# Three more gate projections as seven half-size products, and three small moves after them

## The chip, the cores and the metric

One core of one Trainium2 chip runs one program. The time is device microseconds of that program, the median over several executions. The engines are TensorE (PE in the profile; its weight loads are PEld), VectorE (DVE), ScalarE (ACT), GpSimd (POOL) and SyncE (SP), which here only issues the large weight transfers. Everything is float32.

## What is computed

Two transformer-like blocks run one after the other on a sequence of 256 tokens with 1024 channels. The first block is the one that the change touches:

```python
z = (x @ w_in).astype(F32)
zA, zB, zC, zD, zG = _split(z[..., :N_COLS_BASE], (RWKV_COLS, HGRN_COLS, MLSTM_COLS, LRU_COLS, GATE_COLS))
yA, v_cur = rwkv7_mix(zA, ...)        # four token mixers A, B, C, D
yB, yC, yD = hgrn2_mix(zB, ...), mlstm_mix(zC, ...), rglru_mix(zD, ...)
gates = jax.nn.sigmoid(zG).reshape(bsz, seq, N_BRANCH, D_MODEL)
merged = jnp.zeros((bsz, seq, D_MODEL), F32)
for n, yb in enumerate((yA, yB, yC, yD)):
    merged = merged + gates[:, :, n] * (yb @ w_branch[layer, n])
x = _layernorm(DEEPNORM_ALPHA * x + merged @ w_out[layer], ...)
# then a mixture of 32 experts and a second block with windowed attention
```

## The kernel before

**Units.** The input projection is cut into units of 512 output columns ("B g", "G D 0", "G D 1" and so on; `UNITS`, line 147). A unit's weights are 128 x 8 x 512 floats, 2 MB. They lie in a ring of three places: SP starts the transfer of unit n once unit n-3 has been multiplied (lines 680 to 690, `unit_used`). PE works through the units in the order of the list, and the small matmuls of the four mixers stand between them.

**A unit in the plain form** is `ones_channels` (line 944): two banks of 16 matmuls, each 128 x 128 weights against 256 tokens, 32 in all. ACT copies each bank out (`out`, line 2083).

**A unit in seven products** is Strassen's scheme on 2 x 2 quarters. `early_product` (line 1151) is eight matmuls, 128 x 128 weights against 128 tokens; `early_1` to `early_7` are the seven products P1 to P7 with their waits, 56 matmuls in all. POOL makes the four sums of weight quarters T1 to T4 (`first_sums`, `last_sum`, `in_pieces`, lines 849 to 873), DVE makes the sums of token quarters once for all units (`token_sums`, line 2478). One PSUM bank, U, collects P1, P6, P5 and P3 in turn; ACT copies it out after each (`split_copy`, line 2225: C11 after P1, C21 after P6, C22 after P5, C12 after P3), and DVE adds P2 to C11, P7 to C22 and P7 with P4 to C21 (`c11`, `c22`, `c21`). Four units are done so before: "G B 0", "G B 1", "G A 0", "G A 1" (`EARLY`, line 151). The order in which products, copies and additions are counted is written out in `split_run`, `copy_run` and `add_run` (lines 513 to 523), and must be the order on PE, ACT and DVE.

**The stretch around the three units.** PE runs B i, the small matmul `ada(3)`, B g, the four "C num" banks, G D 0, G D 1, the transposes "C yT", the four banks of `merge("D")` ("Wb D"), "B diag", and then a loop of eight levels with a unit of A between them. ACT and DVE run B's logarithm, its running sum (`tensor_tensor_scan`), and C's normalization at the same time.

**The stretch around the small moves.** A loop `for l in range(1, 5)` builds A's inverse: PE does X{l}, D{l} and DT{l} in 64 x 64 matmuls (lines 1276 to 1311 stand for the small ones of this loop and the merges), with products of G B 0 and G B 1 between them, and DVE copies each result back (lines 2780, 2793, 2803). A table of attention biases for the second block is made on the way, and ACT stores it, 128 times repeated (4.6 MB), to DRAM: `act.dma_start(scratch...)`, line 2223, after the copies of "A Kt". `y_gated` on DVE waits for that store, since its output lies over the table, and SP waits for it before the second block. The bonus term of A is scaled on DVE after X5 (lines 2813 to 2815). At the end of A come G A 0 and G A 1, with the two turns `y_turned(0)` and `y_turned(1)` near the last products, and then `merge("A")`, which needs both halves of A's output ("A_done", from `y_gated`).

Of the kernel before, what the change touches and what calls it, by code (L numbers as in the profile page):

```python
# [7 lines left out]
ALU = mybir.AluOpType  # L8
# [4 lines left out]
P = 128  # L13
# [137 lines left out]
EARLY = ["G B 0", "G B 1", "G A 0", "G A 1"]  # L151
START = len(EARLY)
QKV = [f"{c}{g}" for g in range(GROUPS) for c in "QKV"]
# [66 lines left out]
def build(nc, ins, consts, outs):  # L220
    stack = ExitStack()
    with stack:
# [249 lines left out]
        def split_weights(u):  # L472
# [3 lines left out]
            if u < START:  # L476
                t1, t2, t4 = (room(FREE + 1024 * n, 4, T) for n in range(3))
            elif u > ENDS:
                at_ = RING + SUMS_SLOT * UNIT + u % 2 * 1024
                t1, t2, t4 = room(at_, 4, T), room(at_ + 2048, 4, T), room(FREE + 2048, 4, T)  # L480
            else:
                t1, t2, t4 = spare_w[u % 2]
# [9 lines left out]
        def split_bank(u, which):  # L492
# [6 lines left out]
            else:  # L499
                name = {"U": f"{odd if u % 2 else even} 0", "P2": f"{even} 1", "P7": f"{odd} 1"}[which]  # L500
# [12 lines left out]
        split_run = [(x, u) for u in range(START) for x in ("P1", "P2", "P6", "P7", "P5", "P3", "P4")]  # L513
        split_run += [("P1", START), ("P2", START)] + [x for u in range(START, ENDS + 1) for x in split_turn(u)]
        split_run += [(x, u) for u in LATER for x in ("P1", "P2", "P6", "P7", "P5", "P3", "P4")]
        copy_run = [(x, u) for u in range(START) for x in ("C11", "C21", "C22", "C12")]
# [17 lines left out]
        def split_out(u, i, j):  # L534

            name = SPLIT[u]
            if u < START:
# [282 lines left out]
        def _(pool):  # L820
# [19 lines left out]
            pool.wait_ge(sig("proj_full"), proj_no("A g 1") + 1)  # L840
            for dst, src in ((RELB, ins["rel_bias_2"]), (HOT, consts["hot"]), (TAB, consts["mask"])):
                pool.dma_start(dst, src).then_inc(sig("table_loaded"), 16)
            def mask(l):

                pool.wait_ge(sig("NTm_early"), 4)
                pool.wait_ge(sig("small_full"), small_no(f"A X{l - 1} 1") + 1)
                pool.tensor_tensor(NTm, NT, along(c("level64", l * CH, l * CH + CH), 16), ALU.mult).then_inc(sig("NTm_ready"), 1)

# [25 lines left out]

            mask(2)
            first_sums(0)
            mask(3)
            last_sum(0)
            mask(4)
            first_sums(1)  # L880
            mask(5)
            last_sum(1)
# [4 lines left out]
            for u in range(2, START):  # L887
# [36 lines left out]
        def _(pe):  # L924
# [121 lines left out]
            ones_channels("B g")  # L1046
# [16 lines left out]
            ones_channels("G D 0")  # L1063
            ones_channels("G D 1")
# [10 lines left out]
            turned("C yT", hC.rearrange("p (j h) e -> p j (h e)", j=TT), "C_normed")  # L1075
            merge("D")
# [15 lines left out]
            for l in range(8):  # L1092
# [10 lines left out]
                else:  # L1103
# [3 lines left out]
                    mm.then_inc(sig("small_full"), 1)  # L1107
                if l < 7:
# [41 lines left out]

            def early_product(u, bank, a_name, b_name, first):

                a, b = split_tokens(a_name, SUMS1), split_weights(u)[b_name]
                for m in range(2):
                    for k in range(4):
                        cols = slice(m * P, m * P + P)
                        mm = pe.matmul(split_bank(u, bank)[:, cols], b[:, k, cols], a[:, k, :], start=first and m == 0 and k == 0, stop=k == 3,  # L1157
                                       skip_group_check=True)
                mm.then_inc(sig("split_full"), 1)

            def early_1(u):

                unit(SPLIT[u])
                if u == 0:
                    pe.wait_ge(sig("proj_out"), proj_no("A Kt 1") + 1)
                if u > 1:
                    pe.wait_ge(sig("split_copied"), copied_out("C12", u - 2))
                early_product(u, "U", "A11", "B11", True)

            def early_2(u):  # L1170

                if u:
                    pe.wait_ge(sig("split_added"), added_up("C11", u - 1))
# [2157 lines left out]
```

## Time and profile before

| | |
|---|---|
| median of 3 runs | 1722.17 us (1720.59 to 1722.74) |
| the profiled execution, its own time | 1723.5 us |
| its span in the trace | 1721.7 us |
| PE busy | 1692.8 us, 98% of the span |
| DVE, ACT, POOL busy | 605.9, 271.5, 130.6 us |
| mean granted TensorE clock | 0.998 of full speed |

1.8 us of the profiled time lie outside the span. The timeline lists groups of instructions: start, length, engine, line, operation, sizes, count, and in brackets the idle time before the group and what ended it. A float32 matmul is two records, so 32 matmuls are "x64". Ends of matmuls are modelled and overlap the next start; from start to start is what a group costs.

### The profile page before, as it was taken

The page shows a single profiled execution, that of the slowest core. Times are in us where ns is not written, and L with a number is a line of the kernel's source. Part 1 is how long each engine was busy: PE and PEld are TensorE (multiplying, and loading weights), DVE is VectorE, ACT ScalarE, POOL GpSimd, SP SyncE. Part 2 cuts the span into 40 slices and gives each one's busy share as a digit, 9 for nine tenths or more (in the row PEclk, how much of TensorE's full clock was granted, in tenths as well). Part 3 has the DMA queues.
Part 4 walks back from the last instruction along what each step waited for, and adds up shares of the span by engine and source line. Part 5 has one row for each costly group of instructions (what it writes and reads, how often), then busy time and mean ns, then how long its engine had stood idle before and what let it go on. Part 6 is the DMA issues. An engine that isn't in the chain of part 4 may idle for free.

```text
span 1721.7 us, 25566 instructions
## 1 busy us (share of the span) xinstructions
PE 1692.8 (98%) x10669; PEld 1009.5 (59%) x10669; DVE 605.9 (35%) x1116; ACT 271.5 (16%) x477; POOL 130.6 (8%) x181
## 2 busy tenths in 40 slices
PE   9999999999999999999999999999999999999998
PEld 8787888889553333333434333333333337999995
DVE  4684467456341211111111111112111126454773
ACT  1323115001011111110101010101001112111231
POOL 1000000552000000000000000000000000005600
PEclk9999999999999999999999999999999999999999
DMA  8564332554979999999999999999999997443251
GB/s 320 190 258 166 147 123 100 166 167 185 378 319 423 406 428 428 427 429 428 428 429 428 426 429 427 427 430 427 426 430 427 427 416 297 161 178 117 99 191 48
DMA packets 61975, 540.60 MB, mean 314 GB/s; under 512 B 5192, under 2 KB 12136, under 8 KB 32452
## 3 DMA queue, kind: packets, MB, share of 16 engines
q1 hardware_dynamic: 56160, 528.42, 74.7%
q10 hardware_dynamic: 3956, 5.86, 1.2%
q0 software_dynamic: 1776, 5.10, 0.9%
q8 instruction: 67, 1.10, 0.3%
q14 instruction: 16, 0.13, 0.0%
HBM read 533.57 MB, written 5.78 MB: 313 GB/s over the span
## 4 chain that ended last, share of the span: by engine, by line
PE 92%; DMA 3%; DVE 2%; ACT 1%; issue 1%; SPq 0%; DVEq 0%; ACTq 0%
PE small L1654 24%; PE small L1693 13%; PE proj L1865 11%; PE proj L956 11%; PE proj L1630 3%; PE small L1596 3%; PE proj L1157 3%; PE small L1642 2%; PE small L1661 2%; PE small L976 2%; PE proj L965 2%; PE proj L1140 2%; PE small L1793 2%; PE small L2062 2%; PE small L1519 2%; DMA arena<-in_expert_w_down 1%
## 5 line engine op out<-in xcount | busy, mean ns | idle before, releaser
L1654 PE MATMUL small<-arena 128*64 128x512 f32 x2048 | 446.2, 593 | 2.3 <-DMA arena<-in_expert_w_gu 1.0
L1654 PEld LDWEIGHTS small<-arena 128*64 128x64 f32 x2048 | 151.5, 137 | 281.3 <-issue 276.0
L1693 PE MATMUL small<-arena 128*64 128x512 f32 x1024 | 227.0, 595 | 8.3 <-ACT arena L2288 7.4
L3024 DVE TENSOR_SCALAR arena<-small 128x512 f32<-128x512 f32 x32 | 22.1, 691 | 533.8 <-PE small L1661 533.8
L1865 PE MATMUL proj<-arena 128*128 128x128 f32 x1680 | 192.7, 276 | 0.0
L1865 PEld LDWEIGHTS proj<-arena 128*128 128x128 f32 x1680 | 189.4, 192 | 3.3 <-issue 2.5
L956 PE MATMUL proj<-arena 128*128 128x256 f32 x832 | 183.0, 380 | 0.0
L956 PEld LDWEIGHTS proj<-arena 128*128 128x128 f32 x832 | 157.1, 190 | 22.0 <-issue 0.5
L1693 PEld LDWEIGHTS small<-arena 128*64 128x64 f32 x1024 | 74.3, 137 | 139.5 <-issue 138.4
L852 POOL TENSOR_TENSOR arena<-arena 128x256 f32<-128x256 f32 x144 | 104.5, 759 | 159.3 <-PE proj L1865 98.8
L2283 ACT ACTIVATE arena<-arena 128x512 f32<-128x512 f32 x32 | 20.2, 630 | 490.3 <-DVE arena L3024 490.3
L899 POOL DMA_DIRECT2D arena<-shape_poolcnt x1 | 0.5, 538 | 962.1 <-PE proj L1630 962.1
L2229 ACT ACTIVATE arena<-proj 128x256 f32<-128x256 f32 x76 | 29.1, 383 | 267.6 <-PE proj L1865 161.7
L1630 PE MATMUL proj<-arena 64*128 64x512 f32 x256 | 63.6, 615 | 0.8 <-ACT arena L2323 0.8
L3037 DVE TENSOR_TENSOR arena<-arena 128x128 f32 x16 | 4.7, 292 | 168.1 <-ACT arena L2307 168.1
L1596 PE MATMUL small<-arena 128*64 128x512 f32 x256 | 62.0, 605 | 0.0
L2083 ACT ACTIVATE arena<-proj 128x512 f32<-128x512 f32 (+2 forms) x54 | 30.8, 592 | 186.3 <-PE proj L956 130.8
L2467 DVE TENSOR_TENSOR arena<-proj,arena 128x256 f32<-128x256 f32 x57 | 24.2, 424 | 98.6 <-PE proj L1865 58.5
L1157 PE MATMUL proj<-arena 128*128 128x128 f32 x448 | 55.4, 282 | 0.1
L1157 PEld LDWEIGHTS proj<-arena 128*128 128x128 f32 x448 | 52.6, 196 | 1.2 <-ACT arena L2229 0.3
L2293 ACT ACTIVATE arena<-small 128x512 f32<-128x512 f32 x31 | 18.5, 597 | 208.9 <-PE small L1693 208.9
L3123 DVE TENSOR_TENSOR arena<-arena 128x1024 f32<-128x1024 f32 x40 | 49.0, 1225 | 4.2 <-DVE arena L2467 3.1
(461 smaller groups left out, 1618.3 us busy)
## 6 DMA issues: line engine op xcount, KB each, us to landing
arena<-in_expert_w_gu SPq DMA_DIRECT2D x128, 2048.0 KB, 19.3
arena<-in_expert_w_down SPq DMA_DIRECT2D x47, 2048.0 KB, 27.0
arena<-in_w_in_first SPq DMA_DIRECT2D x20, 2048.0 KB, 8.6
arena<-in_w_in SPq DMA_DIRECT2D x15, 2048.0 KB, 8.1
arena<-in_expert_w_down SPq DMA_DIRECT2D x17, 1536.0 KB, 29.1
arena<-in_w_ada SPq DMA_DIRECT2D x6, 2048.0 KB, 12.7
arena<-in_expert_w_down SPq DMA_DIRECT2D x17, 512.0 KB, 30.7
arena<-in_w_branch SPq DMA_DIRECT2D x4, 2048.0 KB, 8.6
```

The costliest lines, as they stand in the source:

```text
L852: op = pool.tensor_tensor(dst[:, k, :], a[:, k, :], b[:, k, :], ALU.subtract)
L956: mm = pe.matmul(ps[:, m * T:m * T + T], lhs, XT[:, k, :], start=k == 0, stop=k == KD - 1)
L965: mm = pe.matmul(ps[:, :], XT[:, k, j * P:j * P + P], w[:, k, :], start=k == 0, stop=k == KD - 1)
L976: mm = pe.matmul(ps[:, m * T:m * T + T], w[:, k, (2 * i + m) * P:(2 * i + m + 1) * P], YT[b][:, k, :], start=k == 0, stop=k == KW - 1)
L1140: mm = pe.matmul(ps[:, m * T:m * T + T], w[:, k, quarter * P:quarter * P + P], XT[:, k, :], start=k == 0, stop=k == KD - 1)
L1157: mm = pe.matmul(split_bank(u, bank)[:, cols], b[:, k, cols], a[:, k, :], start=first and m == 0 and k == 0, stop=k == 3, skip_group_check ...
L1596: mm = pe.matmul(bank[CAP * half:CAP * half + CAP, :], PICK[:, j, :], x1[:, j, half * W:half * W + W], start=j == 0, stop=j == 1, skip_gro ...
L1630: mm = pe.matmul(acc_bank[2 * j + half][:, :], PTW[lo:lo + CAP, j * P:j * P + P], YSB[lo:lo + CAP, :], start=first, stop=False, skip_group ...
L1654: mm = pe.matmul(bank[CAP * half:CAP * half + CAP, :], XG[:, k % 4, k // 4, :], w[:, k % 4, n * D + half * W:n * D + half * W + W], start= ...
L1693: mm = pe.matmul(bank[CAP * half:CAP * half + CAP, :], h[:, m, u, :], w[:, half * W:half * W + W], start=u == 0 and m == 0, stop=u == 1 an ...
L1865: mm = pe.matmul(split_bank(u, bank)[:, cols], lhs, rhs, start=first and m == 0 and k == 0, stop=k == 3, skip_group_check=True)
L3123: do(TTn(w[dst], w[a], w[b], op), "split_weights")
```

## The change

1. "B g", "G D 0" and "G D 1" go from the plain form to seven products each, with POOL making their weight sums at the point of its queue ahead of the table loads. `token_sums` on DVE moves ahead of B's logarithm. The products of D's two units are staggered: GD1's P1 stands before GD0's P3, and P3 and P4 of the last unit stand behind the turn of C. B g's P3 and P4 stand behind "C num".
2. ACT's store of the bias table moves from behind "A Kt" to behind the gates of G B 1.
3. DVE's scaling of the bonus moves from behind X5 into turn l = 4 of the loop, between the copies of X4 and the addition of D4.
4. The last product P4 of G A 1 moves behind `y_turned(1)` on PE, and on DVE `y_normed(1)` goes ahead of `y_gated(0)` and `c21` of G A 1 behind `y_gated(1)`.

```diff
-EARLY = ["G B 0", "G B 1", "G A 0", "G A 1"]
+EARLY = ["B g", "G D 0", "G D 1", "G B 0", "G B 1", "G A 0", "G A 1"]
...
+            for u in (BG, GD0, GD1):
+                first_sums(u)
+                last_sum(u)
             pool.wait_ge(sig("proj_full"), proj_no("A g 1") + 1)
...
             ones_tokens("B i")
             ada(3)
-            ones_channels("B g")
...
+            early_1(BG)
+            early_2(BG)
+            early_6(BG)
+            early_7(BG)
+            early_5(BG)
             pe.wait_ge(sig("C_weights"), 1)
...
-            ones_channels("G D 0")
-            ones_channels("G D 1")
+            early_3(BG)
+            early_4(BG)
+            early_1(GD0)
+            early_2(GD0)
+            early_6(GD0)
+            early_7(GD0)
+            early_5(GD0)
+            early_1(GD1)
+            early_3(GD0)
+            early_4(GD0)
+            early_2(GD1)
+            early_6(GD1)
+            early_7(GD1)
+            early_5(GD1)
...
             turned("C yT", hC.rearrange("p (j h) e -> p j (h e)", j=TT), "C_normed")
+            early_3(GD1)
+            early_4(GD1)
             merge("D")
...
-            early_3(3)
-            early_4(3)
+            early_3(GA1)
             y_turned(1)
+            early_4(GA1)
             merge("A")
...
             channels("B q", qB)
+            for j in range(TT):
+                out(f"B i {j}", vB[:, j, :])
+            split_copy(BG, "P1", 0, 0)
             act.wait_ge(sig("B_absf"), 1)
             do(act.activation(cB, cB, ACT.Exp, scale=-1.0))
             do(act.activation(cB, cB, ACT.Ln, bias=1.0), "B_ln")
-            for j in range(TT):
-                out(f"B i {j}", vB[:, j, :])
-            channels("B g", gB)
-            act.wait_ge(sig("proj_out"), proj_no("B g 1") + 1)
+            split_copy(BG, "P6", 1, 0)
             do(act.activation(tB, qB, ACT.Sigmoid))
+            split_copy(BG, "P5", 1, 1)
             do(act.activation(kB, fB0, ACT.Sigmoid, scale=-1.0))
+            split_copy(BG, "P3", 0, 1)
+            act.wait_ge(sig("split_copied"), copied_out("C12", BG))
+            act.wait_ge(sig("split_added"), added_up("C21", BG))
             do(act.activation(eB, gB, ACT.Sigmoid), "B_sig")
+            act.nop().then_inc(sig("proj_out"), 2)
+            split_copy(GD0, "P1", 0, 0)
             log_and_exp()
...
+            early_gate(GB1)
             act.wait_ge(sig("table_done"), 1)
             act.dma_start(scratch.rearrange("p h c -> h p c"), along(TAB, P)).then_inc(sig("table_stored"), 16)
...
             dve.nop().then_inc(sig("C_weights"), 1)
+            token_sums(SUMS1)
...
+            c11(BG)
             differences(0)
+            c22(BG)
...
             do(TTn(hC, hC, over(stC[:, 0, :], P), ALU.mult))
+            c21(BG)
...
+                else:
+                    for ct in range(4):
+                        do(STT(bonusA[:, ct, :], bonusA[:, ct, :], pv("rwkv_lnx_b", ct, ct + 1), gA[:, ct, :], ALU.add, ALU.mult))
+                    do(TTn(gA, gA, over(pv("rwkv_lnx_g"), T), ALU.mult))
                 for i in range(TT):
                     do(TTn(Dv[:, i], tiles(full(f"A D{l} {i}"), CH), Dv[:, i], ALU.add), "small_out")
...
-            y_gated(0)
             y_normed(1)
-            c21(3)
+            y_gated(0)
             y_gated(1)
+            c21(GA1)
             merge("A", False)
```

## Rows read from the trace of the kernel before

**Rows 1.** The page: the busy time of the engines.

```profile
PE 1692.8 (98%) x10669; PEld 1009.5 (59%) x10669; DVE 605.9 (35%) x1116; ACT 271.5 (16%) x477; POOL 130.6 (8%) x181
```

**Rows 2.** Waits of PE up to 480 us: waiter, releaser, us, times, longest.

```profile
PE small L1300 <- issue: 3.2, 1, 3.2
PE small L976 <- DVE arena L2886: 1.6, 1, 1.6
PE small L1300 <- DVE arena L2749: 0.8, 1, 0.8
```

**Rows 3.** Timeline of PE: B g, and what follows it.

```profile
141.75 14.06 PE L956 MATMUL proj<-arena 128*128 128x256 f32 x64
155.65 1.06 PE L1057 MATMUL small<-arena 128*128 128x129 f32 x8
```

**Rows 4.** Timeline of PE: two of the seven products, and what follows them.

```profile
328.00 3.84 PE L1157 MATMUL proj<-arena 128*128 128x128 f32 x32
331.67 1.04 PE L1311 MATMUL small<-arena 128*128 128x128 f32 x8
```

**Rows 5.** Timelines of DVE, ACT and POOL: what the three units' chain is made of.

```profile
147.08 2.87 DVE L2619 TENSOR_TENSOR_SCAN arena<-arena 128x256 f32<-128x256 f32 x4
...
159.89 1.22 DVE L2645 TENSOR_TENSOR arena<-arena 128x1024 f32<-128x1024 f32 x1
...
143.57 1.06 ACT L2152 ACTIVATE arena<-arena 128x1024 f32<-128x1024 f32 x1 [18.19 <-DVE arena L2615]
...
330.15 0.38 ACT L2229 ACTIVATE arena<-proj 128x256 f32<-128x256 f32 x1 [23.52 <-PE proj L1157]
...
408.27 12.20 POOL L852 TENSOR_TENSOR arena<-arena 128x256 f32<-128x256 f32 x16 [33.56 <-PE proj L1157]
```

**Rows 6.** Timeline of PE around the longest gap, in turn l = 4.

```profile
353.45 1.04 PE L1300 MATMUL small<-arena 64*64 64x64 f32 x54
...
358.34 3.37 PE L1157 MATMUL proj<-arena 128*128 128x128 f32 x16
361.55 1.04 PE L1311 MATMUL small<-arena 128*128 128x128 f32 x8
```

**Rows 7.** Windows: each engine's busy us (instructions), PEclk, DMA share, GB/s.

```profile
330.00:340.00 10.00, 10.00 (x185) 9.69 (x186) 3.33 (x7) 1.15 (x3) 2.42 (x2) 1.00 0.86 284
...
380.00:390.00 10.00, 10.00 (x251) 8.75 (x251) 6.54 (x12) 0.00 (x0) 0.00 (x0) 1.00 0.01 3
...
358.00:359.00 1.00, 1.00 (x13) 0.88 (x10) 0.64 (x1) 0.00 (x0) 0.00 (x0) 0.50 1.09 354
```

**Rows 8.** Timeline of ACT: the issue of the bias table's store.

```profile
323.66 0.35 ACTq L2223 DMA_DIRECT2D bias_rows<-arena  x1
```

**Rows 9.** DMA, 344 to 345 and 366 to 367: weight loads, KB each, us to landing.

```profile
arena<-in_w_in_first SPq DMA_DIRECT2D x1, 2048.0 KB, 15.9
...
arena<-in_w_in_first SPq DMA_DIRECT2D x1, 2048.0 KB, 8.5
```

**Rows 10.** DMA queues, 354 to 358 and 358 to 362: packets, MB, share.

```profile
q8 instruction: 1, 0.02, 1.4%
...
q10 hardware_dynamic: 211, 0.31, 20.5%
```

**Rows 11.** Timeline of DVE: the bonus, the same operation elsewhere, the copies of X4.

```profile
216.32 1.01 DVE L2687 SCALAR_TENSOR_TENSOR arena<-arena 128x256 f32<-128x256 f32 x2
...
349.88 1.42 DVE L2780 COPY arena<-small 128x512 f32<-128x512 f32 x2 [0.69 <-PE small L1289]
...
368.82 3.63 DVE L2814 SCALAR_TENSOR_TENSOR arena<-arena 128x256 f32<-128x256 f32 x4
372.49 1.63 DVE L2815 TENSOR_TENSOR arena<-arena 128x1024 f32<-128x1024 f32 x1
```

**Rows 12.** Timeline of DVE ahead of `merge("A")`.

```profile
427.89 0.69 DVE L2879 TENSOR_TENSOR arena<-arena 128x512 f32<-128x512 f32 x1
...
429.79 0.42 DVE L2467 TENSOR_TENSOR arena<-proj,arena 128x256 f32<-128x256 f32 x1 [1.21 <-PE proj L1157]
```

More of the change, by code:

```diff
@@ L499, in split_bank @@
             else:
-                name = {"U": f"{odd if u % 2 else even} 0", "P2": f"{even} 1", "P7": f"{odd} 1"}[which]
+                name = {"U": f"{odd if (u - START) % 2 else even} 0", "P2": f"{even} 1", "P7": f"{odd} 1"}[which]
             return proj_bank[proj_no(name) % 4]
@@ L885, in _ @@
             pool.dma_start(bcb, ins["ln1_b"][0].partition_broadcast(P)).then_inc(sig("ln1_loaded"), 16)
-            for u in range(2, START):
+            for u in (GA0, GA1):
                 first_sums(u)
@@ L1045, in _, with early_product @@
             ada(3)
-            ones_channels("B g")
+            def early_product(u, bank, a_name, b_name, first):
+                a, b = split_tokens(a_name, SUMS1), split_weights(u)[b_name]
+                for m in range(2):
+                    for k in range(4):
+                        cols = slice(m * P, m * P + P)
+                        mm = pe.matmul(split_bank(u, bank)[:, cols], b[:, k, cols], a[:, k, :], start=first and m == 0 and k == 0, stop=k == 3,
+                                       skip_group_check=True)
+                mm.then_inc(sig("split_full"), 1)
@@ new lines, in early_5, with early_3, early_4 @@
+            def early_5(u):
+                pe.wait_ge(sig("split_copied"), copied_out("C21", u))
+                early_product(u, "U", "S1", "T1", False)
+            def early_3(u):
+                pe.wait_ge(sig("split_copied"), copied_out("C22", u))
+                early_product(u, "U", "S4", "B22", False)
+            def early_4(u):
+                pe.wait_ge(sig("split_weights"), 4 * u + 4)
+                pe.wait_ge(sig("split_added"), added_up("C22", u))
+                early_product(u, "P7", "A22", "T4", False)
+                for _ in range(2):
+                    pe.nop().then_inc(sig("proj_full"), 1)
@@ L2809, in _ @@
                     dve.nop().then_inc(sig("table_done"), 1)
[L2810 removed]
+            c21(GB1)
             for i in range(TT):
                 do(TTn(X[:, 8 * i:8 * i + 8, :], tiles(full(f"A X5 {i}"), CH), along(c("eye64"), 8), ALU.add), "small_out")
[L2813 to L2815 removed]
             merge("B", False, (0,))
```

261 lines of the change are left out of this document (132 added, 129 removed).

## The prediction

> **What bounds the kernel now.** First the page: PE is busy for 1692.8 us of a span of 1721.7, and the next engine for 605.9 [rows 1]. So the time is PE's work plus its gaps, 28.9 us in all. An edit pays if it shortens PE's work or closes a gap of PE; work on any other engine costs nothing until PE waits for it. Second, the waits of PE in the first 480 us, where the whole change lies: 3.2 us on "issue" (nothing that the trace shows), 1.6 us for the last half of A's output, and 0.8 us for a copy behind the bonus [rows 2]. Third, the timeline of PE around B g: the groups follow one another with no idle time [rows 3], so there only PE's own work can be saved, and every new wait is paid in full.
>
> **Seven products for three units.** A plain unit of 64 records runs from 141.75 to 155.65, that is 13.90 us [rows 3]. Two products of eight matmuls, 32 records, run from 328.00 to 331.67, that is 3.67 us or 1.835 each [rows 4]; seven are 12.85. The saving is 1.05 us a unit, 3.15 for three. It is small because half the tokens per matmul don't give half the time (0.229 us against 0.434): seven eighths of the arithmetic would be 12.16, and 0.69 us of each unit is lost to the shorter matmul.
>
> What the products wait for, by hand from 141.75. POOL needs 12.2 us for the four sums of a unit [rows 5]. Those of B g start when its weights land, about 136, and are done before the products that read them. Those of G D 0 start with the end of B g's P5 (141.75 + 5 x 1.835 = 150.9) and T2 is there after half of them, at 157.0, while PE comes to P6 of G D 0 only at 141.75 + 9 x 1.835 + 2.7 for "C num" = 160.9. So POOL hides, with 4 us to spare. For G D 1 the spare is 7.3 - 6.1 = 1.2 us: four products lie between P5 of G D 0 and P6 of G D 1.
>
> DVE and ACT are the tighter chain. ACT can copy P1 of G D 0 out only after B's last sigmoid, which now needs the whole of B g, its last addition C21 among it, and DVE does that addition only after B's logarithm and C's division. From 142.2 on DVE: token sums 2.8 (four of 512 elements, at 1.22 for 1024 [rows 5]), absolute value 1.2, then ACT 2 x 1.1 [rows 5], then DVE 1.2, scans 2.9 [rows 5], C11 0.4, differences 1.4, C22 0.4, eight copies of "C num" 2.4, small ones 0.8, the division 1.2, C21 0.5: 159.8 to 160.3. ACT's sigmoid 1.1 and the copy 0.4 [rows 5] give 161.8 to 162.1. PE wants it at 160.9, so P6 of G D 0 waits about 1.1 us. Behind it on PE stands everything else, so it is paid. The lower bound is 0.9. The upper one takes each of some six two-operand operations of that chain longer by 0.4, as the bonus is at 368.82 while POOL works (0.908 each against 0.505) [rows 11]: 3.5. I take 1.2, since POOL is idle in most of that chain (B g's sums end near 148). Later copies, C's turn and the gates of D have several us of room, and D's merge follows as before. Sum of part 1: -3.15 + 1.2 = **-1.9** (-2.3 to +0.4).
>
> The page "SBUF — State Buffer" of the Trainium skill, section "SBUF: two separate sides", says that a DVE operation with two SBUF inputs and a GpSimd one lock each other out for a whole instruction. Rows 11 agree with it (0.4 us more each). By it every unit's 16 POOL operations could hold DVE up; the sum above is bounded by the rows and doesn't need it.
>
> **The store of the bias table.** ACT issues it at 323.66 [rows 8]; 211 of its packets still move between 358 and 362 [rows 10]. While it runs, a weight load takes 15.9 us to land, and one issued at 366 takes 8.5 [rows 9]. In the midst of one group of D4, after 54 of 64 records, PE stands still for 3.24 us on "issue" [rows 2, 6]. No semaphore stands inside that group, and the next packet of the instruction queue is the one that moves between 354 and 358 [rows 10]: I read it as PE out of instructions, whose fetch is behind the store and the stretched weight load. The clock then goes from 1.00 to 0.50 (2.4 to 1.2 GHz) [rows 7], and a product takes 3.21 us instead of 1.835 [rows 6], 1.4 more. The gap and its clock are **4.6 us**. With the store issued some 44 us later (about 367, behind G B 1's gates), that place has a load of 8.5 us only. I take all 4.6 as gained there; the other end is 0, if the weight load alone is enough.
>
> The store is moved, not removed. It then runs from about 368 to 395, at first beside the load of G A 1, which is needed at 414 and has room, and PE's instructions go faster there: 251 records in 380 to 390 against 185 in 330 to 340 [rows 7]. Something of the same kind may come back. Bounds are 0 (with the store and a load together at 330 to 340, DMA share 0.86, PE had no gap [rows 7]) and 4.6 once more; I take **+0.7**. The wait of DVE for the store in `y_gated`, at about 427, has 30 us of room, and `merge("B")` and the loads behind are not queued on ACT. ACT's queue gains nothing else.
>
> The page "Runtime: NRT & Kernel Launch", section "Instruction fetch mechanics", of the Trainium skill says that instructions come in blocks of 16 KiB by a queue of the engine's own, and that a crossing is mostly hidden. By that rule the gap of 3.24 us would have another cause and part 2 would be worth 0. Rows 6 and 10 speak against "hidden": one packet of the instruction queue falls into the gap.
>
> **The bonus sooner.** The four operations and the multiplication take 3.63 + 1.63 = 5.3 us with POOL busy, 4 x 0.505 + 1.2 = 3.2 without [rows 11]. At their new place DVE is free from 351.3 (end of the copies of X4, 349.88 + 1.42 [rows 11]) until PE ends D4. POOL is busy there too. So DVE ends at 354.5 to 356.6, and the two additions of D4 (1.4) at 356.1 to 358.1. PE runs D4 from 353.45 for 1.1 and one product of 1.8 behind it, and wants the result at 356.4: a new wait of 0 to 1.8, and behind it on PE stand DT4 and all the rest. I take **+1.2**. At the old place the wait of 0.8 goes [rows 2]: **-0.8**. Next late there is PE itself, with no gap before 431.
>
> **The last product behind the second turn.** PE waits 1.6 us for A_done before `merge("A")` [rows 2]. On DVE, C21 of G A 1 at 429.79 waited 1.21 us for P4 with the last `y_gated` behind it, and `y_normed(1)` at 427.89 stood behind `y_gated(0)` [rows 12]. Now DVE does the norm at about 426.5, PE turns it after P3, near 427.8, and P4 fills the next 1.8 us while DVE does four operations of 0.7, done near 430.0, just as P4 ends. **-1.5** (-1.6 to -0.8). The addition C21 and its sigmoid are late by 2 us, but the merge needs that half of the gate only 7 us later.
>
> **Sum**: -1.9 - 4.6 + 0.7 + 1.2 - 0.8 - 1.5 = -6.9 us. The profiled execution of 1723.5 becomes 1716.6, and the median of 1722.2 becomes 1715.3 us. The profiled execution is 1.3 above the median; I keep the difference and not its time.
>
> **Rivals.**
> (a) The fetch gap comes back once under the moved store, or stays at 354 because the load alone makes it. For it: PE's instructions are denser there [rows 7], and I can't see from outside where a block ends. Against it: the store ran beside a load at 330 to 340 with no gap. -6.9 - 0.7 + 4.6 = -3.0: 1719.2. The rule of the Runtime page leads to the same time by another way.
> (b) The three units cost more than they save: the chain over B g's C21 is longer, because POOL's sums stretch DVE's operations, or G D 1's sums come late (1.2 us of room). The wait is then 3.5 for the first and about 2 for the second, part 1 is +2.4 instead of -1.9, and the time 1719.6.
> (c) Slower: the gap comes back several times. The place is 372 to 395, where PE uses its instructions 251/185 = 1.36 times as fast with the store in every DMA engine's queue. At 4.6 us each, three of them give -7.6 + 13.8 = +6.2: 1728.4. It decides from 11.0 us of new gaps on (7.6 to make good, 3.4 for the bound). Against it: even in the old place there was one gap in 38 us of store.
> (d) The moves don't do what they say: the clock and the gap are a matter of one execution and not of the median. The three runs spread over 2.2 us, less than the 4.6, so the gap is in all or in none; if it is in none, -2.3: 1719.9.
>
> **Chances.** Forecast 0.58; (a) 0.18; (b) 0.08; (c) 0.06; (d) 0.10. What this kernel's measurement can tell from no change is about 0.2%, 3.4 us: faster is below 1718.7. The forecast's own range, 1712.0 (no wait anywhere: -3.15 + 0.9 - 4.6 - 0.8 - 1.6, less 1 for what I can't see) to 1718.7, is faster; of (a), (b) and (d), whose centres lie 1 us on the other side, about one in six is. Faster 0.63, same 0.30, slower 0.07. The range that should hold it 8 times in 10 takes in those three centres with 2 us above them: 1712.0 to 1721.7.
>
> **What would show each step.** Seven products of about 1.83 us for each of the three units, with one gap of about 1 us before P6 of G D 0, released by ACT's copy; "C yT" and "Wb D" start 2 us sooner. No "issue" gap near 350, PEclk 1.00 from 350 to 362, and the load of G A 0 landing in 8.5 us. A gap of about 1 us before DT4, released by DVE. No wait before DT5, and at most 0.3 before `merge("A")`. It is wrong if an "issue" gap of over 2 us stands between 365 and 400, if DVE's operations near 150 to 160 are much above their lengths of rows 5, or if a weight load after 366 makes PE wait.

## The result: slower by 0.6%, and the profile after

The changed kernel takes 1732.43 us (median of 4 runs, 1729.07 to 1734.59) against 1721.38 for the kernel before (4 runs, 1719.80 to 1722.74): a ratio of 1.0064, 95% interval 1.0052 to 1.0076, that is 9.0 to 13.1 us. The forecast was 1715.3 with a range of 1712.0 to 1721.7. The profiled execution is the shortest of the four, 1729.07 us with a span of 1727.3.

First the waits of PE up to 480 us, which answer to [rows 2] (waiter, releaser, us, times, longest):

```profile
PE small L1454 <- issue: 2.9, 1, 2.9
PE proj L1062 <- ACT arena L2190: 2.6, 1, 2.6
PE small L1347 <- DVE arena L2856: 1.8, 1, 1.8
PE proj L1062 <- issue: 1.6, 1, 1.6
PE proj L1062 <- POOL arena L850: 1.6, 1, 1.6
PE proj L1062 <- DVE arena L2517: 1.5, 1, 1.5
...
PE small L1508 <- issue: 0.9, 1, 0.9
PE proj L1062 <- DVE arena L2531: 0.3, 1, 0.3
```

The three waits of [rows 2] were 5.6 us together. They are gone from their places, and eight others of 13.2 us stand there. Five of them are L1062, the seven products of the three units. The timeline of PE behind B g's first five products, which answers to [rows 3]:

```profile
154.73 1.95 PE L1062 MATMUL proj<-arena 128*128 128x128 f32 x16
158.19 5.60 PE L1062 MATMUL proj<-arena 128*128 128x128 f32 x48 [1.52 <-DVE arena L2517]
166.42 14.37 PE L1062 MATMUL proj<-arena 128*128 128x128 f32 x112 [2.63 <-ACT arena L2190]
182.40 2.02 PE L1062 MATMUL proj<-arena 128*128 128x128 f32 x16 [1.61 <-issue]
185.98 3.84 PE L1062 MATMUL proj<-arena 128*128 128x128 f32 x32 [1.56 <-POOL arena L850]
189.66 1.04 PE L1161 MATMUL small<-arena 128*128 128x128 f32 x8
190.53 3.74 PE L1062 MATMUL proj<-arena 128*128 128x128 f32 x32
194.10 6.21 PE L986 MATMUL small<-arena 128*128 128x256 f32 x28
```

Read the gaps by what stands behind them: 158.19 is P4 of B g, waiting for the addition C22; 166.42 is P6 of G D 0, waiting for ACT's copy of its P1; 182.40 is P6 of G D 1 (the wait has no releaser in the records; in the experiment without sums below it is gone) and 185.98 its P7, waiting for POOL's T2 and T3. The merge of D begins at 194.10, 51.9 us behind B g's start (142.19), where it was 45.1. And the later part, with a window of 395 to 398 (busy us of PE, PEld, DVE, ACT, POOL with instructions, PEclk, DMA share, GB/s):

```profile
365.66 1.09 PE L1347 MATMUL small<-arena 128*128 128x128 f32 x8 [1.78 <-DVE arena L2856]
...
398.08 1.27 PE L1454 MATMUL small<-arena 64*64 64x64 f32 x34 [2.86 <-issue]
...
437.66 2.64 PE L986 MATMUL small<-arena 128*128 128x256 f32 x11
...
395.00:398.00 3.00, 0.21 (x7) 0.08 (x3) 0.67 (x1) 0.00 (x0) 0.00 (x0) 1.00 0.94 238
```

The gap near 355 [rows 6] is gone, and one of the same kind, in the midst of a group of 64 records and with the DMA queues full, stands at 398. The merge of A at 437.66 has no wait any more.

### The profile page after: what moved, and what is told of

It is laid out like the page before. It is cut to its first block, busy times and chain, and to the rows that moved or that the text cites. A ratio compares the mean times of both kernels' runs of the same rounds, so it can differ in the third digit from the quotient of the medians.

```text
span 1727.3 us, 25957 instructions
## 1 busy us (share of the span) xinstructions
PE 1691.2 (98%) x10813; PEld 1011.5 (59%) x10813; DVE 615.4 (36%) x1125; ACT 274.4 (16%) x485; POOL 169.7 (10%) x229
## 4 chain that ended last, share of the span: by engine, by line
PE 91%; DVE 4%; DMA 1%; ACT 1%; issue 1%; POOL 1%; DVEq 0%; ACTq 0%; POOLq 0%
PE small L1690 25%; PE small L1729 13%; PE proj L1901 11%; PE proj L966 8%; PE proj L1666 3%; PE small L1632 3%; PE proj L1062 3%; PE small L1678 2%; PE small L1697 2%; PE small L1312 2%; PE small L986 2%; PE proj L975 2%; PE proj L1233 2%; PE small L1829 2%; PE small L2098 2%; PE small L1555 2%
## 5 line engine op out<-in xcount | busy, mean ns | idle before, releaser
L1901 PE MATMUL proj<-arena 128*128 128x128 f32 x1680 | 192.7, 276 | 0.0
L850 POOL TENSOR_TENSOR arena<-arena 128x256 f32<-128x256 f32 x192 | 143.6, 781 | 203.3 <-PE proj L1901 101.0
L966 PE MATMUL proj<-arena 128*128 128x256 f32 x640 | 141.0, 380 | 0.0
L1062 PE MATMUL proj<-arena 128*128 128x128 f32 x784 | 95.3, 280 | 7.7 <-ACT arena L2190 2.6
L1062 PEld LDWEIGHTS proj<-arena 128*128 128x128 f32 x784 | 91.1, 195 | 9.8 <-issue 6.2
L2190 ACT ACTIVATE arena<-proj 128x256 f32<-128x256 f32 x88 | 33.7, 383 | 293.4 <-PE proj L1901 161.7
L2517 DVE TENSOR_TENSOR arena<-proj,arena 128x256 f32<-128x256 f32 x66 | 28.0, 425 | 106.6 <-PE proj L1901 58.9
L2119 ACT ACTIVATE arena<-proj 128x512 f32<-128x512 f32 (+2 forms) x48 | 27.3, 591 | 174.3 <-PE proj L966 103.7
## 6 DMA issues: line engine op xcount, KB each, us to landing
arena<-in_w_ada SPq DMA_DIRECT2D x6, 2048.0 KB, 12.2
```

The costliest lines, as they stand in the source:

```text
L850: op = pool.tensor_tensor(dst[:, k, :], a[:, k, :], b[:, k, :], ALU.subtract)
L966: mm = pe.matmul(ps[:, m * T:m * T + T], lhs, XT[:, k, :], start=k == 0, stop=k == KD - 1)
L1901: mm = pe.matmul(split_bank(u, bank)[:, cols], lhs, rhs, start=first and m == 0 and k == 0, stop=k == 3, skip_group_check=True)
```

## The experiments

Two theories at first. **P**: the three units lose by POOL's sums, which are late themselves and stretch DVE's operations. **F**: the moved store starves PE of instructions at its new place. The texts written ahead of the runs also name rivals: **W**, the whole loss is PE's new waits between 142 and 190 us; **Q**, the order of ACT's and DVE's queues makes them; **M**, the moved bonus makes the loss of the three moves. The kernels ran in three groups of four, in the order of the table, each group on one chip (three chips in all) beside the kernel before; it took 1721.11 (26 runs), 1721.17 (31) and 1720.85 us (26).

| kernel | median us (lowest to highest, runs) | ratio, 95% interval |
|---|---|---|
| the three moves alone | 1727.58 (1721.01 to 1731.06, 10) | 1.0036, 1.0021 to 1.0051 |
| the products alone | 1727.14 (1725.31 to 1729.05, 5) | 1.0038, 1.0024 to 1.0053 |
| products, no sums on POOL | 1718.54 (1716.24 to 1719.56, 10) | 0.9987, 0.9978 to 0.9997 |
| products, queues reordered | 1721.62 (1719.17 to 1725.68, 10) | 1.0006, 0.9996 to 1.0015 |
| store alone | 1725.79 (1719.12 to 1729.86, 10) | 1.0027, 1.0009 to 1.0045 |
| bonus alone | 1720.44 (1719.25 to 1723.36, 10) | 0.9994, 0.9980 to 1.0007 |
| last product alone | 1718.13 (1716.99 to 1722.87, 10) | 0.9988, 0.9977 to 0.9999 |
| three moves, store of 32 rows | 1720.95 (1720.05 to 1722.26, 10) | 1.0002, 0.9992 to 1.0012 |
| before, store of 32 rows | 1718.87 (1718.16 to 1720.07, 10) | 0.9992, 0.9983 to 1.0002 |
| two units | 1716.99 (1714.58 to 1720.10, 10) | 0.9978, 0.9966 to 0.9991 |
| two units, store of 32 rows | 1714.66 (1714.33 to 1715.32, 7) | 0.9966, 0.9954 to 0.9977 |
| the change, store of 32 rows | 1723.67 (1722.75 to 1726.17, 8) | 1.0020, 1.0009 to 1.0031 |

### The two halves of the change

The three moves (store, bonus, last product) on the kernel before; and the changed kernel with the three moves undone. Both are cut from the diff of the change as it stands; of the first, the store:

```diff
                 out(f"A Kt {i}", Kt[:, i, :])
-            act.wait_ge(sig("table_done"), 1)
-            act.dma_start(scratch.rearrange("p h c -> h p c"), along(TAB, P)).then_inc(sig("table_stored"), 16)
...
             early_gate(1)
+            act.wait_ge(sig("table_done"), 1)
+            act.dma_start(scratch.rearrange("p h c -> h p c"), along(TAB, P)).then_inc(sig("table_stored"), 16)
             act.wait_ge(sig("merged"), 3)
```

> The kernel before with the three later moves alone (store later, bonus sooner, last product behind the second turn); no unit is changed. Theory W (the loss comes from PE's new waits between 142 and 190 us, and the moves gain a little): the profiled span falls by about 1.3 us against 1721.7, since from 328 to 431 the changed kernel ran 1.34 us shorter than the one before (lead of 7.28 us at the first product of G B 0, 5.94 at the merge of A), and the median lies 0.5 to 2.5 us below before's. Theory F (the moved store leaves PE without instructions in another place in each execution, and this makes the median of the changed kernel worse by 11 us where its profiled execution is worse by 5.6): the median is 3 to 6 us above before's, and the trace has an 'issue' gap of 2 to 6 us between 365 and 400.

> The three units as seven products, and none of the three later moves. Theory W: the merge of D starts 7.3 us later than in the kernel before (194.1 against 186.8), as in the changed kernel, with the waits 0.3, 1.5, 2.6, 1.6 and 1.6 us on PE before it; the span and the median are 6 to 8 us above before's, and the 3.2 us gap on issue stands in the loop as it did or at another place nearby. Theory F: the median is only 5 to 7 us above, and the rest of the 11 us is missing because the store is back at its old place.

Measured: +6.5 and +6.0 us. Each half loses by itself, and together they are near the change's +11. In the profile of the moves alone the gap on "issue" is 3.30 us, at another place (381.73), and the executions lie 10 us apart. In that of the products alone the merge of D comes 50.3 us behind B g's start.

### The products without POOL's sums

```diff
-                in_pieces(w["T1"], w["B12"], w["B11"])
+                in_pieces(w["T1"], w["B12"], w["B11"], u < GB0)
```

> The three units as seven products without the later moves, and POOL's sums of weights for these three units left out (each sum is one memset of one column instead of four subtractions; the products read rooms that are not sums). Theory P (POOL is the cause: its sums come late for G D 1, and its work stretches DVE's operations): the waits of PE on POOL (1.6 us twice) go, DVE's operations between 150 and 185 have their old lengths (differences 0.69, the division 1.22), the chain of B g's C21 is about 3 us shorter, and of the 7.3 us lead at the merge of D 5 to 7 go. Theory Q (the order of the queues is the cause: ACT's copy of G D 0 stands behind a sigmoid that wants the whole of B g, and DVE's addition C22 stands behind the scans and the differences): the waits of 1.5 and 2.6 us stay at over half their size, and only the two on POOL go: the lead falls by about 3.5 us.

`u < GB0` sets the argument `light` of `in_pieces` for the three units: one small memset then stands in place of the four operations of each sum. The products read rooms that hold no sums, so this kernel doesn't compute the block; it is built for its times alone.

The timeline of PE, and two rows of DVE (the differences of B):

```profile
162.01 18.10 PE L1067 MATMUL proj<-arena 128*128 128x128 f32 x160 [1.22 <-ACT arena L2195]
...
184.40 1.89 PE L991 MATMUL small<-arena 128*128 128x256 f32 x8
...
153.17 0.69 DVE L2688 TENSOR_TENSOR arena<-arena 128x512 f32<-128x512 f32 x1
153.90 0.69 DVE L2689 TENSOR_TENSOR arena<-arena 128x512 f32<-128x512 f32 x1
```

With POOL idle one gap is left, 1.22 us ahead of P6 of G D 0, and the stretch takes 184.40 - 141.58 = 42.8 us, 2.3 less than before. The gaps ahead of P6 and P7 of G D 1 are gone with the sums. POOL's sums, and what they stretch on DVE, are all that was taken out, so the wait of P6 is put down to T2, though the records name no releaser. Theory P holds for the products: the same instructions on PE gain 2.3 us without POOL's work and lose 5.2 with it. What POOL does to DVE stands in the trace of the changed kernel:

```profile
151.06 3.64 DVE L2670 TENSOR_TENSOR_SCAN arena<-arena 128x256 f32<-128x256 f32 x4
...
155.19 1.27 DVE L2683 TENSOR_TENSOR arena<-arena 128x512 f32<-128x512 f32 x1
156.49 1.10 DVE L2684 TENSOR_TENSOR arena<-arena 128x512 f32<-128x512 f32 x1
...
158.28 0.42 DVE L2692 COPY arena<-small 128x256 f32<-128x256 f32 x1
...
160.90 0.72 DVE L2695 SCALAR_TENSOR_TENSOR arena<-arena 128x8 f32<-128x8 f32 x1
...
162.57 1.59 DVE L2698 TENSOR_TENSOR arena<-arena 128x1024 f32<-128x1024 f32 x1
...
164.72 1.06 ACT L2213 ACTIVATE arena<-arena 128x1024 f32<-128x1024 f32 x1 [7.56 <-DVE arena L2517]
165.89 0.38 ACT L2190 ACTIVATE arena<-proj 128x256 f32<-128x256 f32 x1
...
152.36 13.76 POOL L850 TENSOR_TENSOR arena<-arena 128x256 f32<-128x256 f32 x16 [8.11 <-PE proj L1062]
173.79 14.99 POOL L850 TENSOR_TENSOR arena<-arena 128x256 f32<-128x256 f32 x16 [7.68 <-PE proj L1062]
```

The differences take 1.27 and 1.10 us instead of 0.69, the scans 3.64 instead of 2.87 [rows 5], an operation of eight elements 0.72 instead of 0.17 (another, at 158.08, keeps its 0.17), and POOL's 16 operations 13.8 and 15.0 instead of 12.2 [rows 5]. The copies out of PSUM at 158.28 keep their 0.42. The page "SBUF — State Buffer" of the Trainium skill, section "SBUF: two separate sides", says that a DVE operation with two SBUF inputs and a GpSimd one that reads SBUF keep each other out for a whole instruction. The trace agrees: the operations above that grew have both inputs in SBUF, and the copies have none there.

### Queues reordered

ACT copies P1 of G D 0 ahead of B's last sigmoid; DVE does B g's additions C11 and C22 ahead of B's logarithm and differences, and C21 ahead of C's division. Nothing is added or removed.

```diff
+            split_copy(GD0, "P1", 0, 0)
             act.wait_ge(sig("split_copied"), copied_out("C12", BG))
             act.wait_ge(sig("split_added"), added_up("C21", BG))
             do(act.activation(eB, gB, ACT.Sigmoid), "B_sig")
             act.nop().then_inc(sig("proj_out"), 2)
-            split_copy(GD0, "P1", 0, 0)
```

> The three units as seven products without the later moves, POOL's sums as they are, and the queues put in another order: ACT copies P1 of G D 0 ahead of B's last sigmoid, DVE does C11 of B g in its idle time before B's logarithm, C22 ahead of the differences, and C21 ahead of C's division. Theory Q: the waits of 1.5 and 2.6 us go, with the half clock behind the second one (about 1.4 us), and the merge of D starts about 5 us earlier than in the run with the products alone; the waits on POOL stay or grow, since the sums of G D 1 still start with the end of P5 of G D 0. Theory P: other waits of the same size take their place, and the merge of D starts less than 2 us earlier.

```profile
170.91 5.62 PE L1062 MATMUL proj<-arena 128*128 128x128 f32 x48 [2.42 <-ACT arena L2190]
177.03 2.02 PE L1062 MATMUL proj<-arena 128*128 128x128 f32 x16 [0.49 <-issue]
181.07 3.84 PE L1062 MATMUL proj<-arena 128*128 128x128 f32 x32 [2.01 <-POOL arena L850]
...
189.19 3.19 PE L986 MATMUL small<-arena 128*128 128x256 f32 x14
```

The gaps of 1.52 and 2.63 us are gone, and one of 2.42 is there in their place: ACT's copy of P5 stands behind its wait for C's variance, as it did before the reordering, and PE now comes to it first. From B g's start (141.70) to the merge of D it is 47.5 us, 2.8 less than with the products alone, still 2.4 more than before. G D 1 still waits for its sums; an order of queues doesn't help that.

### The moves one by one

On the kernel before, the store as in the diff above; the bonus:

```diff
-                if l == 3:
+                elif l == 3:
                     c22(0)
+                else:
+                    for ct in range(4):
+                        do(STT(bonusA[:, ct, :], bonusA[:, ct, :], pv("rwkv_lnx_b", ct, ct + 1), gA[:, ct, :], ALU.add, ALU.mult))
+                    do(TTn(gA, gA, over(pv("rwkv_lnx_g"), T), ALU.mult))
...
-            for ct in range(4):
-                do(STT(bonusA[:, ct, :], bonusA[:, ct, :], pv("rwkv_lnx_b", ct, ct + 1), gA[:, ct, :], ALU.add, ALU.mult))
-            do(TTn(gA, gA, over(pv("rwkv_lnx_g"), T), ALU.mult))
             merge("B", False, (0,))
```

and the last product, on PE and then on DVE:

```diff
             early_3(3)
-            early_4(3)
             y_turned(1)
+            early_4(3)
...
-            y_gated(0)
             y_normed(1)
-            c21(3)
+            y_gated(0)
             y_gated(1)
+            c21(3)
```

> The kernel before with one move alone: the store of the bias table is issued behind G B 1's sigmoid (about 364 instead of 324 us). Nothing else is changed. Theory F (PE runs out of instructions behind the store, once or more, wherever the store runs): a gap of PE on "issue" of 2 to 4 us at a new place between 370 and 395, none near 354; a median some 4 to 7 us above before, about 1726 (1723 to 1730), and executions that lie several us apart, as with the three moves together (1721.0 to 1731.1). Rival M (the loss of the three moves is that of the bonus and of what waits behind it): 1721 or, with the old gap of 4.6 us closed, down to 1716.5, and executions within 3 us.

> The kernel before with the scaling of the bonus alone moved to the fourth turn of the loop. It takes PE's wait of 0.8 us at DT5 away and makes one of about 1.8 us before DT4 (measured with the three moves together). Theory F: +1.0, so 1722.1 (1721 to 1723.5), executions within 3 us of each other. Rival M: 1725 or more, with another wait of PE behind it.

> The kernel before with the product P4 of G A 1 alone moved behind the second turn of y. The wait of 1.6 us before the merge of A goes, and nothing takes its place: -1.5 us, 1719.6 (1719 to 1720.5). Rival: the merge waits for the gate's half that now comes 2 us later, or nothing is gained because the merge's weights or DVE are as late: 1721.1.

The store alone is the loss of the three moves: +4.6 us in the median, with executions from 1719.1 to 1729.9. The profiled execution (1723.15) shows one large gap (a second is 0.17) and, in the window behind it, the granted clock near half (1.2 of 2.4 GHz):

```profile
377.04 0.41 PE L1398 MATMUL small<-arena 64*64 64x64 f32 x8
380.60 3.14 PE L1398 MATMUL small<-arena 64*64 64x64 f32 x53 [3.14 <-issue]
...
382.00:384.00 2.00, 2.00 (x47) 2.00 (x45) 0.73 (x2) 0.00 (x0) 0.00 (x0) 0.53 0.75 169
```

The bonus alone (-0.7) can't be told from no change. In its trace neither wait of DVE stands: a gap on "issue" of 1.86 in D4 lies over the bonus. The last product alone gives -3.0 in the median with an interval from -4.0 to -0.2; its wait of 1.6 us is gone, and -1.6 lies within the interval.

### A smaller store

The table's 128 rows in memory are all the same row; the load reads each one column further back. Four loads of 32 partitions, each with its own start, need 32 rows: 1.2 MB to store and not 4.7 (128 rows of 24 x 384 floats; the 4.6 MB given at the start is a little low).

```diff
-            act.dma_start(scratch.rearrange("p h c -> h p c"), along(TAB, P)).then_inc(sig("table_stored"), 16)
+            act.dma_start(scratch.rearrange("p h c -> h p c"), along(TAB, 32)).then_inc(sig("table_stored"), 16)
...
-                    tab = bass.AP(tensor=scratch.tensor, offset=P - 1, ap=[[24 * BKT - 1, P], [BKT, 24], [1, T]])
-                    sp.dma_start(HK, tab).then_inc(sig("hankel_loaded"), 16)
+                    for a in range(4):
+                        tab = bass.AP(tensor=scratch.tensor, offset=P - 1 - 32 * a, ap=[[24 * BKT - 1, 32], [BKT, 24], [1, T]])
+                        sp.dma_start(HK[32 * a:32 * a + 32], tab).then_inc(sig("hankel_loaded"), 16)
```

> The three moves as in the run with all of them, but the moved store writes 32 rows of the bias table instead of 128 (1.2 MB instead of 4.7), and four loads of 32 partitions read them later; the result is the same table. Theory F: with a store of some 7 to 10 us in place of 27 PE's instructions come in time: no gap on "issue" over 1 us between 350 and 400, so -4.6 (the old gap) +1.0 (bonus) -1.5 (last product) = -5.1, about 1716 (1715 to 1719), and executions within 3 us of each other. Rival: the gaps aren't the store's but those of the place (64x64 matmuls use up instructions too fast) or of the bonus's wait: about 1727 as with the full store, or at least a gap of 2 us or more in the profile.

The waits of PE, up to 480 us and behind:

```profile
PE small L1312 <- DVE arena L2798: 1.8, 1, 1.8
...
PE proj L1866 <- DMA arena<-in_w_in: 1.7, 1, 1.7
```

No gap on "issue" between 350 and 400, and the executions lie 2.2 us apart and not 10: as theory F has it. The median, 1720.95, is 5 us above the 1716 expected. 1.7 us of it is a new wait: the four loads hold SP for 4.23 us at 1434, with a weight load behind them. Most of the rest is that I had counted the old gap at its 4.6 us from before's median, where it is not worth that much; the next run shows how much. There and from there on the four loads stand behind that weight load.

> The kernel before with the store at its old place (about 324 us) but of 32 rows instead of 128, read by four loads that are issued behind the next weight load and not ahead of it. Theory F (the gap of 3.2 us near 355 comes of the 4.7 MB store): no gap of PE on "issue" over 1 us between 340 and 400, the profiled span shorter by 3.2 + 1.4, so near 1717; the median, where the gap is of different size from one execution to the next, at about the lowest of before's executions, 1718.5 (1717.5 to 1719.5), and executions within 3 us. Rival (the weight load alone makes the gap, or the place): the gap stays, 1721.2 with the spread of before.

The waits of PE up to 480 us:

```profile
PE small L977 <- DVE arena L2887: 1.6, 1, 1.6
PE small L991 <- DVE arena L2484: 1.2, 1, 1.2
PE small L1301 <- DVE arena L2750: 0.8, 1, 0.8
```

(L991's 1.2 is at the start of the kernel and stands in the kernel before too.) No gap on "issue", and 1718.16 to 1720.07 us in place of 1718.46 to 1725.94. So the large store makes the gap, not the weight load beside it. In the median it comes to 2.0 us (1720.85 to 1718.87); the interval of the ratio is -2.9 to +0.3 us, which excludes 4.6 and does not exclude 0. What is clear is the narrower spread.

Where the gaps stand is not chance. Counted from the start of each trace, they come after these numbers of matmul records (each has one weight load):

| kernels | records ahead of the gap | its length, us |
|---|---|---|
| before; last product; bonus | 2486 | 3.24; 2.79; 1.86 |
| three moves; store alone | 2864 | 3.30; 3.14 |
| last product; store alone | 3369 | 0.29; 0.17 |
| products alone; no sums; reordered | 2606 | 2.01; 1.46; 1.15 |
| the change | 3238 | 2.86 |
| the change; no sums; reordered; the change with 32 rows | 3490 | 0.86; 0.90; 0.36; 0.35 |
| two units | 2357 and 2608 | 2.50 and 0.53 |

Kernels with the same instructions up to that point have the gap at the same record, and within one list of instructions the places lie about 126 records, or a multiple of it, apart (378, 505, 632, 252, 251). In all 17 cases PE starts again 1.3 to 1.7 us after the end of a 16 KB packet of the queue "q8 instruction". That is what PE out of instructions looks like: the possible places are fixed by the program, and the transfers under way decide whether a gap opens there and how long it is. The four small ones at record 3490 show that a gap of up to 0.90 us also comes without the table's store: in the run without sums only weight loads and the instruction packet move from 398 to 401.2, ahead of the gap's end at 401.16.

### Two units, and the change with a small store

The version that the runs point to: B g and G D 0 as seven products, G D 1 plain, with its first half between P5 and P3 of G D 0; the queues as above, and ACT's copy of P5 ahead of its wait for C's variance; the last product moved; the bonus and the store where they were.

```diff
-            early_1(GD1)
+            ones_channels("G D 1", (0,))
             early_3(GD0)
             early_4(GD0)
-            early_2(GD1)
-            early_6(GD1)
-            early_7(GD1)
-            early_5(GD1)
+            pe.wait_ge(sig("split_copied"), copied_out("C12", GD0))
+            ones_channels("G D 1", (1,))
```

> A version without the loss: B g and G D 0 as seven products, G D 1 plain as before, with ACT's and DVE's queues in the order of the run with reordered queues and ACT's copy of P5 ahead of the wait for C's variance; the last product of G A 1 behind the second turn; the store of 128 rows and the bonus at their old places. Half of G D 1 lies between P5 and P3 of G D 0. Theory P (what the products lose is waiting for POOL's sums and for DVE's and ACT's chain beside them): B g's start to merge D takes 45.1 - 2 x 1.05 = 43.0 us, at most 0.8 more; with the last product's -1.6 the sum is -3.7 us, 1717.5 (1716.5 to 1719), with the gap near 355 still there. Rival: products cost PE more than their seven times 1.835 us even without a wait, or POOL's sums stretch DVE so that new waits come: 45 us or more to merge D, and 1719.5 or more.

> The kernel of the run two_units, with the store of 32 rows and its four later loads as in before_quarter. If the gap belongs to the large store and the two edits add, 1717.5 - 2.7 = 1714.8 (1713.5 to 1716.5), executions within 3 us, no gap on "issue" over 1 us between 340 and 400. Rival: the gap goes elsewhere, since the block ends of PE's instructions have moved: as two_units, 1717.5.

> The changed kernel whole, with one thing different: the moved store is of 32 rows instead of 128, and four loads behind the next weight load read them. It splits the loss of the change. Theory F: what the store costs goes, some 6.6 us as between the three moves with the full and with the small store (1727.6 and 1721.0), and 1.7 us of a late weight load don't come back: 1732.4 - 7.5 = 1725 (1723.5 to 1727); the products' part of the loss, about +6, stays. No gap on "issue" over 1 us between 360 and 400. Rival (the store's cost in the changed kernel is small; the late sums and the chain carry all of the loss): 1730 or more.

PE in the run with two units:

```profile
142.22 3.82 PE L1062 MATMUL proj<-arena 128*128 128x128 f32 x32
146.35 5.90 PE L1062 MATMUL proj<-arena 128*128 128x128 f32 x48 [0.31 <-DVE arena L2523]
...
154.78 12.67 PE L1062 MATMUL proj<-arena 128*128 128x128 f32 x112
167.28 7.07 PE L966 MATMUL proj<-arena 128*128 128x256 f32 x32
174.19 3.73 PE L1062 MATMUL proj<-arena 128*128 128x128 f32 x32
...
185.54 13.98 PE L986 MATMUL small<-arena 128*128 128x256 f32 x64
```

From 142.22 to 185.54 it is 43.3 us, where 43.0 to 43.8 was expected, and the one gap is 0.31. In the profiled execution, the longest of the ten, an "issue" gap of 2.50 us stands at 341.79 and one of 0.53 at 360.38: the store is still the large one. With the small store they go, and the median is 1714.66 us, 6.2 below the kernel before, all seven executions within 1 us of each other. It beats both kernels.

The changed kernel with the small store takes 1723.67, 8.8 us less than with the large one. Its first stretch ends, from B g at 141.91:

```profile
166.22 12.74 PE L1063 MATMUL proj<-arena 128*128 128x128 f32 x112 [2.63 <-ACT arena L2191]
...
192.28 7.94 PE L987 MATMUL small<-arena 128*128 128x256 f32 x36
```

That closes the account without the gap: 50.4 us against 45.1 is +5.3 for the products, +1.0 for the bonus (1.8 comes, 0.8 goes), -1.6 for the last product, +4.7 in all; measured between the two kernels with the small store +4.8 (1718.87 to 1723.67).

## Why the prediction was wrong

**What bounds the kernel** was read rightly: what was lost or won is PE's own work and its gaps in the first 480 us.

**The three units: -1.9 forecast, +5.2 to +5.3 measured** (+6.8 in the profiled execution, where the clock fell behind the gap of 2.63). The saving on PE was right. The waits were not, and two steps of the working failed.
- "I take 1.2, since POOL is idle in most of that chain (B g's sums end near 148)." My own working had G D 0's sums start at 150.9 and run 12 us, over the end of that chain. In the trace they run from 152.36 to 166.1, beside DVE's scans and all that follows, and B g's own sums end at 144.3, sooner than the 148 that I took, but beside the token sums. Five stretched places, against the run without sums, (token sums 0.64, scans 0.77, differences 0.99, two small ones 1.03, division 0.36) make 3.8 us, and the sigmoid begins at 164.72 and not at about 160. P6 of G D 0 waits 2.63, and P4 of B g waits 1.52 ahead of it for C22, which DVE's queue holds behind the two differences; that second place I hadn't walked through at all. The range's upper end, six operations longer by 0.4, was 3.5 for this; it was 4.2. The walk was also added up wrongly: its terms give 159.6 for C21 and 161.1 for ACT's copy, a wait of 0.2 and not 1.1. With POOL idle the wait was 1.22, so the 1.1 is near the truth by luck.
- "For G D 1 the spare is 7.3 - 6.1 = 1.2 us." 6.1 is half of POOL's 12.2 us with DVE idle or elsewhere. Here DVE works beside it and 16 sums take 15.0, so T2 is ready after some 7.5, and four products don't cover it: 1.61 and then 1.56 for T3. The change asks DVE and POOL for more work in one and the same stretch, so neither's length from a quiet stretch holds.

Rival (b) had this mechanism and its price, +2.4, was too low.

**The moved store: -4.6 + 0.7 forecast, +4.6 measured in the median.** Two steps failed. The first is a size: the gap of [rows 6] was taken at its 4.6 us from the median, because three executions lay only 2.2 us apart. In groups of 26, 31 and 26 they lie 6.0, 9.5 and 7.5 apart, and making the store small in its place gives 2.0 us in the median. The second is the choice of 0.7 between 0 and 4.6. I let the stretch of 330 to 340, with no gap, speak against one between 365 and 400; it doesn't, since a gap can only stand where a block of PE's instructions ends, and ten quiet microseconds say little of the next such place. "I can't see from outside where a block ends" was wrong too: the records can be counted, as above. The length then varies at one and the same place (1.86 to 3.24 us at record 2486). Against a kernel without the large store, the moved one costs 6.9 us in the median (1718.87 to 1725.79) and up to 11.0 in one execution. The two kernels ran on different chips, where the kernel before differs by 0.3 us. Rival (c) named the place (372 to 395), the reason and +6.2, and got 0.06. The page "Runtime: NRT & Kernel Launch" of the Trainium skill, section "Instruction fetch mechanics", has such crossings "mostly hidden"; in the kernels with the 1.2 MB store that agrees (the largest such gap before 480 us is 0.35), with the 4.7 MB store it doesn't (3.30).

**The bonus: +1.2 - 0.8 forecast**, +1.8 - 0.8 in the trace: the wait before DT4 is 1.78, the upper end of 0 to 1.8. **The last product: -1.5 forecast**, the wait of 1.59 gone and nothing in its place. Both steps held, the second within its range and the first at its edge. With the bonus alone the gap on "issue" hid both of its waits, so the +1.0 is seen only in the kernels that have no such gap in D4.

**The sum**: 5.3 + 4.6 + 1.0 - 1.6 = +9.3 against +11.0 measured. The interval of the +11.0 is 9.0 to 13.1, so the 1.7 between them need not be anything; if it is something, it lies with the store, since the same sum without the store closes (+4.7 against +4.8). Making the store small gives 8.8 us in the changed kernel, 6.6 in the one with the three moves (8.3 without that kernel's late load), and 6.9 lie between the store alone and the kernel before with a small one. What exactly the long executions lose is open: every profiled execution with the moved store is one of its kernel's shorter ones, with one gap of 2.9 to 3.3 us and at most a second of 0.86. That there are several large gaps in the long ones, as in rival (c), is argued and not seen.

## What to carry to other kernels

Work put on an idle engine isn't free when it runs beside the engine of the critical chain: price both at the lengths they have side by side, and redo the walk with them. A gap of PE with no releaser, in the midst of one group and beside a large transfer, is a hint at instructions that come late: count the matmul records ahead of it, and look for a packet of the instruction queue just before its end. Here moving the transfer moved the gap, and making it smaller removed it. And the size of such a gap is that of one execution: look at the spread of many before its price is taken from a median.

## What the runs showed of the hardware that I had not expected

- The executions of one kernel spread with the size of one store: 1.0, 1.9, 2.2 and 3.4 us with 1.2 MB in the four kernels that have it; with 4.7 MB 6.0 to 9.5 us in the three groups of the kernel before, and 10.0 and 10.7 with the store moved. The two ranges meet: it is 3.3 in the run without sums, with the large store.
- A DVE operation of only eight elements takes 0.72 us instead of 0.17 beside POOL's sums: the added 0.55 is as much as the added time of one with 128x512 (0.41 and 0.58), so it isn't a share of its own work. Not each one is hit: that at 158.08 takes 0.17.
- The granted clock falls behind some gaps and not behind others of the same length: after 2.63 us ahead of P6 of G D 0 it was 0.78 of full in one execution (165 to 170), between the levels of 1.2 and 2.4 GHz in the mean, and the next 112 records took 14.37 us; with the same gap in the run with the small store it was 1.00 and they took 12.74.
- Up to 480 us the gaps of PE on "issue" in the midst of a group stand only at places about 126 matmul records, or a multiple of it, apart, and end 1.3 to 1.7 us after a packet of the instruction queue.
- Four loads of 32 partitions in place of one of 128 hold SP's queue 4.23 us and not 0.38, and a weight load behind them made PE wait 1.7 us.
